# Forgetting-attention scores: one f32 product replaced by three fp32r products of upper and lower parts, on one Trainium2 core

## The reference, cut to what matters

```python
def forgetting_attention(q, k, v, f_logit, b_f):
    qh = q.reshape(bsz, s, FOX_HEADS, FOX_HEAD_DIM)      # 4 heads of 128
    kh = k.reshape(bsz, s, FOX_HEADS, FOX_HEAD_DIM)
    vh = v.reshape(bsz, s, FOX_HEADS, FOX_HEAD_DIM)
    cum = jnp.cumsum(jax.nn.log_sigmoid((f_logit + b_f).astype(jnp.float32)), axis=1)
    ...
        logits = jnp.einsum('bqhd,bshd->bhqs', qb, kh).astype(jnp.float32) * (FOX_HEAD_DIM ** -0.5)
        logits = logits + jnp.transpose(cq, (0, 2, 1))[..., None] - cum_k[:, :, None, :]
        logits = jnp.where((key_pos[None, :] <= pos_q[:, None])[None, None], logits, -jnp.inf)
        p = jax.nn.softmax(logits, axis=-1).astype(vh.dtype)
        o = jnp.einsum('bhqs,bshd->bqhd', p, vh)
```

## Time and profile before

| | |
|---|---|
| median of 3 runs | 1112.43 us |
| profiled execution | 1112.43 us |
| its span | 1110.5 us |
| TensorE (PE) busy | 1100.7 us, 99% of the span |
| VectorE (DVE) busy | 743.5 us, 67% |
| ScalarE (ACT) busy | 507.2 us, 46% |
| mean granted TensorE clock | 0.999 of full speed |

### The profile page before, as it was taken

The page is one execution under the profiler, slowest core; times in us unless marked ns, Lnnn a source line. Parts: engine busy times, 40 slices in busy tenths (PEclk is TensorE's granted clock), DMA queues, the critical chain, the costliest instruction groups (busy, mean ns, idle before and its releaser), DMA issues. The chain is left out here.

```text
span 1110.5 us, 18066 instructions
## 1 busy us (share of the span) xinstructions
PE 1100.7 (99%) x7342; PEld 931.0 (84%) x7344; DVE 743.5 (67%) x1195; ACT 507.2 (46%) x851; POOL 19.8 (2%) x40
## 2 busy tenths in 40 slices
PE   9999999999999999999999999999999999999997
PEld 8888888888888888878888787887789999999986
DVE  6875876864686147448789896447558687667853
ACT  7662354324675325543352434336544444444543
POOL 1000000000001001000000000000000000000000
PEclk9999999999999999999999999999999999999999
DMA  9643324432215333522223222131112322333241
GB/s 372 220 149 125 124 69 133 127 101 72 75 58 172 134 101 108 182 75 77 77 76 95 76 95 73 61 114 58 57 58 76 114 87 86 115 115 114 77 190 76
DMA packets 33618, 121.09 MB, mean 109 GB/s; under 512 B 3824, under 2 KB 3824, under 8 KB 33536
## 3 DMA queue, kind: packets, MB, share of 16 engines
q1 hardware_dynamic: 30672, 109.88, 29.4%
q0 software_dynamic: 2720, 10.03, 2.6%
q10 hardware_dynamic: 144, 0.03, 0.0%
HBM read 115.74 MB, written 4.19 MB: 108 GB/s over the span
## 5 line engine op out<-in xcount | busy, mean ns | idle before, releaser
L1160 DVE TENSOR_TENSOR w_lo<-raw,w_hi 128x1024 fp32r<-128x1024 f32 (+2 forms) x194 | 225.8, 1165 | 149.3 <-ACT w_hi L649 146.5
L1826 PE MATMUL acc<-hT_hi,w_hi 128*128 128x512 f32 x648 | 259.0, 400 | 0.0
L1828 PE MATMUL acc<-hT_hi,w_lo 128*128 128x512 f32 x648 | 252.9, 390 | 0.0
L1827 PE MATMUL acc<-hT_lo,w_hi 128*128 128x512 f32 x648 | 252.4, 389 | 0.0
L649 ACT ACTIVATE w_hi<-raw 128x1024 fp32r<-128x1024 f32 (+2 forms) x194 | 195.5, 1009 | 114.3 <-PE acc L1828 85.5
L1826 PEld LDWEIGHTS acc<-hT_hi,w_hi 128*128 128x128 f32 x648 | 121.9, 188 | 27.0 <-issue 3.1
L1828 PEld LDWEIGHTS acc<-hT_hi,w_lo 128*128 128x128 f32 x648 | 121.6, 188 | 26.1
L1827 PEld LDWEIGHTS acc<-hT_lo,w_hi 128*128 128x128 f32 x648 | 121.9, 188 | 23.6
L1826 PE MATMUL acc<-w_hi,hT_hi 128*128 128x512 f32 (+1 forms) x152 | 60.3, 397 | 0.0
L1828 PE MATMUL acc<-w_hi,hT_lo 128*128 128x512 f32 (+1 forms) x152 | 58.8, 387 | 0.0
L1827 PE MATMUL acc<-w_lo,hT_hi 128*128 128x512 f32 (+1 forms) x152 | 58.7, 386 | 0.0
(11 more groups left out here) (461 smaller groups left out, 2250.3 us busy)
## 6 DMA issues: line engine op xcount, KB each, us to landing
raw<-in_ga SPq DMA_DIRECT2D x32, 512.0 KB, 4.5
ada_raw<-in_ada SPq DMA_DIRECT2D x16, 512.0 KB, 11.6
raw<-in_wo SPq DMA_DIRECT2D x16, 512.0 KB, 3.5
raw<-in_br SPq DMA_DIRECT2D x16, 512.0 KB, 3.5
raw<-in_q SPq DMA_DIRECT2D x8, 512.0 KB, 3.5
raw<-in_u SPq DMA_DIRECT2D x8, 512.0 KB, 3.8
raw<-in_gp SPq DMA_DIRECT2D x8, 512.0 KB, 4.6
raw<-in_ada_w SPq DMA_DIRECT2D x8, 512.0 KB, 3.5
```

The lines of the kernel that those rows point to most:

```text
L1160: nc.vector.tensor_tensor(out=lo[:, 0:width], in0=strip_of(k), in1=hi[:, 0:width].bitcast(f32), op=ALU.subtract).then_inc(lo_made, 1)
L1826: nc.tensor.matmul(ps, w[0], x[0], start=first, stop=False)
L1827: nc.tensor.matmul(ps, w[0], x[1], start=False, stop=False)
L1828: return nc.tensor.matmul(ps, w[1], x[0], start=False, stop=last)
```

## The change

The queries and keys of the forgetting attention are kept as upper and lower parts, and the score is made of three fp32r matmuls in place of one f32 matmul. ScalarE's copies of dq and dk now write fp32r upper parts and no longer free the bank. VectorE makes the lower part, bank minus upper part, and frees the bank with it. It waits for ScalarE's copy with the new semaphore `fox_hi_made`. Two further waits protect the memory that `fox_k_lo` takes over. The bias rows `forget` move to another address.

```diff
-BY_DVE = ("gp", "gh", "pw", "az", "bz", "cz", "dz", "cx", "cb", "br", "w2")
+BY_DVE = ("gp", "gh", "pw", "az", "bz", "cz", "dz", "cx", "cb", "dq", "dk", "br", "w2")
...
-        fox_q, fox_k = at("fox_q", M, [P, 4, S]), at("fox_k", M + 8192, [P, 4, S])
+        fox_q_hi, fox_q_lo = at("fox_q_hi", M, [P, 4, S], f32r), at("fox_q_lo", R_MP, [P, 4, S], f32r)
+        fox_k_hi, fox_k_lo = at("fox_k_hi", M + 8192, [P, 4, S], f32r), at("fox_k_lo", M + 24576, [P, 4, S], f32r)
...
-        forget = at("forget", M + 24576, [4, 2, S])
+        forget = at("forget", R_MP + 12288, [4, 2, S])
...
                 if kind == "dq":
-                    copy_out(fox_q[:, j, :], r, freed["act"], scale=float(P) ** -0.5)
+                    copy_out(fox_q_hi[:, j, :], r, fox_hi_made, scale=float(P) ** -0.5)
                 if kind == "dk":
-                    copy_out(fox_k[:, j, :], r, freed["act"])
+                    copy_out(fox_k_hi[:, j, :], r, fox_hi_made)
...
+                if kind == "dq":
+                    dve.wait_ge(fox_hi_made, j + 1)
+                    nc.vector.scalar_tensor_tensor(out=fox_q_lo[:, j, :], in0=acc[r % 4][:, :], scalar=float(P) ** -0.5,
+                                                   in1=fox_q_hi[:, j, :].bitcast(f32), op0=ALU.mult, op1=ALU.subtract)\
+                        .then_inc(freed["dve"], 1)
+                if kind == "dk":
+                    dve.wait_ge(fox_hi_made, 5 + j)
+                    if j == 1:
+                        dve.wait_ge(summed, SPARSE)
+                    if j == 2:
+                        dve.wait_ge(turned, BANK2.index(("up", TT - 1)) + 1)
+                    nc.vector.tensor_tensor(out=fox_k_lo[:, j, :], in0=acc[r % 4][:, :], in1=fox_k_hi[:, j, :].bitcast(f32),
+                                            op=ALU.subtract).then_inc(freed["dve"], 1)
...
-                    nc.tensor.matmul(ps[:, 0:w], fox_q[:, h, tok], fox_k[:, h, 0:w], start=True, stop=False)
+                    nc.tensor.matmul(ps[:, 0:w], fox_q_hi[:, h, tok], fox_k_hi[:, h, 0:w], start=True, stop=False)
+                    nc.tensor.matmul(ps[:, 0:w], fox_q_hi[:, h, tok], fox_k_lo[:, h, 0:w], start=False, stop=False)
+                    nc.tensor.matmul(ps[:, 0:w], fox_q_lo[:, h, tok], fox_k_hi[:, h, 0:w], start=False, stop=False)
```

More of the change, by code:

```diff
@@ L449, in program @@
         latq_made, latq_copied = sem("latq_made"), sem("latq_copied")
+        fox_hi_made = sem("fox_hi_made")
         logits_made, max_made, exp_made, probs_made = sem("logits_made"), sem("max_made"), sem("exp_made"), sem("probs_made")
```

## The result

| | before | after |
|---|---|---|
| median of 14 runs | 1112.44 us | 1115.39 us |
| lowest to highest | 1112.29 to 1112.57 | 1113.93 to 1115.81 |
| profiled execution, its span | 1112.43, 1110.5 us | 1115.8, 1112.1 us |

The ratio is 1.0023, 95% interval 1.0016 to 1.0030: slower, by 3.0 us, which is 0.3%. The prediction was 1113.6 with a range up to 1114.9.

The account below looks back on a forecast made before the run. TensorE, busy 99% of the span, was taken to bound the kernel. Scores at -1.18 us and a new wait of +2.32 us gave +1.14 on 1112.43, so 1113.6 us; range 1111.2 to 1114.9.

Parts of the forecast that it names:

- What bounds the kernel: TensorE, busy 99% of the span; only what shortens, lengthens or stops its queue moves the end.
- The scores: Three fp32r products per score on TensorE: 1.52 us less at widths 512 to 256, 0.34 more at 128; 1.18 less in all.
- what slot 39 swallows: Width 128 scores: 0.10 us idle before slot 39's next turning absorbs 0.10 of the 0.44 us loss, leaving 0.34.
- VectorE's steps up to dk 1: VectorE's new lower parts from dq 0 to dk 1, 0.69 us each: all hidden, no cost to TensorE.
- The division of s = 13: Behind dq 0, slot 28: moves back by 0.69 us, hidden with 2.2 us to spare before TensorE wants it.
- The wait at dk 3: Slot 35: VectorE frees the bank late, so tile 3 of dv 0 starts at 722.97, not 720.65: new wait of 2.32 us.
- The clock: TensorE's pause in dv 0: half-level clock might cost some 1.5 us more; left out of the sum, given chance 0.08.
- The rival: The pause of 2.3 us in dv 0 costs clock, some 1.5 us more: 1115.1 us; chance 0.08.

## Why the prediction was wrong, step by step

- **What bounds the kernel: right.** TensorE's busy time is unchanged and the end moved with its waits.
- **The scores: the mechanism right, the size too large.** By width, the prices were right within 0.02: 0.70 and 0.52 for three products at 512 and 384, 0.36 at 256, and 0.11 for each product at width 128. The sum of 1.18 should have been 0.68. I counted what slot 39 swallows and didn't ask the same of slots 40 to 43, where the turning behind the score waits for the copy as well and 0.40 is given back. This term alone moves the forecast from 1113.6 to 1114.1, inside the range and on the lower level.
- **VectorE's steps up to dk 1: right.** The division of s = 13 starts at 672.65 in place of 672.00 and nothing follows from it.
- **The wait at dk 3: right to the tenth.** Forecast 2.32 us from two queues laid side by side; measured 2.0 us of idle time and 2.32 in the chain, 2.27 without the 0.05 from before.
- **The clock: this is the step that failed.** The sum holds the pause at its length, 2.32 us, and its cost in clock at nothing. The rival had the mechanism, its place and its price (1.5 us, and 1115.1 as its time; the upper level is at 1115.4 to 1115.8, the rest being the scores). I gave it 0.08 because no pause of this length stood in full work in the trace, and cut the range short of it at 1114.9. Absence of a pause is no evidence that a pause is free, and the only rows that bore on it spoke for the cost. The runs show it in 12 of 20 spans with a pause of 2.0 us, at some 1.5 us each. And I wrote of it as of something that either happens or not; it is a chance in each execution, so a median depends on how many of its executions it hits.
- The range would have held the lower level (1113.95). With seven of 14 spans on each level, that the median came out on the upper one is partly chance: the two times that exceed their spans by 3.1 and 3.7 us put it there.

## What to carry to other kernels

When an accumulator's release moves from one engine to another, look up what stands ahead of it in the new engine's queue at the last result of each group, not at the average one: here the closest of the first seven releases, that of dk 2, came at 712.08 us, some 7 us before TensorE wanted the bank, and the eighth stood behind a serial chain of 8.8 us. If a change makes the bounding engine pause for some 2 us in full work, price the pause twice, once as itself and once as a stretch at half clock; moving the chain by one slot avoids both. A saving between two steps that are tied to another engine's copy is not a saving; check each place where it falls, and whether another step binds once the first is moved.

The best version found is the change with the bias chain one slot later and ScalarE's copy first: 1110.79 us, 1.7 us below the kernel before. Of that 1.0 is the order of the copies, which has nothing to do with the change, and 0.7 the change itself. Of these differences only the 1.7 is clear of the interval (ratio 0.9986, 0.9977 to 0.9995).

## What the runs showed of the hardware

- A pause of 2.0 us in otherwise full work left the clock at 1.00 in one profile and was followed in another by 3.4 us (723.55 to 726.9) of granted clock 0.50, with matmuls at 0.43 in place of 0.23 us; spans with it are 1.3 to 1.7 us longer. With pauses of 1.1 us no span of 11 shows it. A pause of 3.4 us left the clock at 1.00 in the one profile of it, while four of the five spans are longer.
- fp32r products of width 128, each with its own weights, stand 0.11 us apart, no closer than those of width 256 at 0.12.
- Open: some times exceed the span recorded with them by 2.9 to 3.7 us where 1.9 to 2.1 is usual: two of 14 in the changed kernel, two of 11 with the pause of 1.1 us, two of 11 and one of 11 with the chain moved (with the old and the new order of copies). Every one is of a kernel with the three products and none of the pause filled (0 of 11) or lengthened (0 of 5); kernels with f32 products have none in the 55 executions of the kernel before taken beside the experiments, nor in 6, 11 and 11 of the others. One profile, that of the changed kernel, is of such an execution (1115.8, span 1112.1), and its trace shows nothing unusual. So the cause is open.
